# Latent attention in a decoder layer: one exponential over four key blocks, in a pair of PSUM banks

## The chip, the cores and the metric

The kernel runs on all 8 cores of one Trainium2 chip. Each core computes one eighth of the tokens: four cores share a batch element, and each of them owns 16 of its 64 blocks of 128 tokens. The cores don't talk to each other. The metric is the device time in microseconds of the slowest core.

Engines as the profile names them: PE is the matrix engine (PEld its weight loads), ACT is ScalarE, DVE is VectorE, POOL is GpSimd, SP issues the DMAs.

## What is computed

The reference is a decoder layer: RMS norm, one input projection, four retention heads beside eight heads of multi-head latent attention (MLA), an output projection, a SwiGLU feed-forward part and a gated per-layer embedding. The change touches the attention alone, which is this, for each of the 8 heads (query and key 96 wide, value 64 wide, sequence 8192):

```python
s = jnp.einsum('bhqd,bhkd->bhqk', qi, kt).astype(jnp.float32) * scale
mask = kpos[None, :] <= qpos[:, None]
s = jnp.where(mask[None, None], s, -1e30)
pr = jax.nn.softmax(s, axis=-1).astype(vt.dtype)
return jnp.einsum('bhqk,bhkd->bhqd', pr, vt)
```

## The kernel before

**How the program is written.** One Python function, `build_program`, emits five instruction streams. Every operation names the buffers that it reads and writes, and a small tracker adds a semaphore wait where a buffer's last writer or reader is on another engine. Each engine runs its own stream strictly in the order in which the program adds operations. The eight PSUM banks (128 partitions x 512 fp32) are eight separate buffers, `banks[0]` to `banks[7]`; `bank()` (L332) hands out banks 0 to 5 in turn. All matmuls are recorded at L361, in the helper `MM`, whatever they compute, so that they are told apart by shape.

**Stages.** First input projection and retention; then the attention, which is what the change touches, about 1.0 ms; then output projection, feed-forward and embedding, behind a barrier.

**Attention.** The outer loop runs over 4 pairs of heads (`hp`). For each pair it projects keys, values and queries of both heads (L880 to L923), and then works through *rounds*: a round is one head `a` (0 or 1) and one group `g` (0 to 7) of 256 own queries. A round covers `nkb = 8 * (g + 1)` key blocks of 128; the last 8 of them lie at the diagonal and get a mask. There are 64 rounds, with 2304 key blocks in all.

A round is cut into *steps* of two key blocks. For each step:

- `emit_S`: for each block one matmul 96*128, 96x256 (scores, transposed: keys on partitions, 256 queries along the row), into half a bank. For a masked block a second matmul 128*128, 128x256 adds the mask to it.
- `emit_rest`: one exponential on ACT (L963) over the bank, 128x512 from PSUM into a bf16 tile `PTS[t % 4]`; then for each block one matmul 128*65, 128x256 that accumulates values times probabilities (and, in row 64, the denominator) in `acc`, bank 6 or 7.
- Behind a round's last step: a copy of `acc` on ACT (L968), and a reciprocal of the one row of denominators on DVE (L969).
- `emit_F2`, some steps later: one fp32 matmul 1*64, 1x256 (two passes on PE) that spreads the reciprocal over 64 partitions, into a bank from `bank()`, and a multiply on DVE (L953 or L956) that reads it.

The order on PE comes from this loop, where `LOOK = 2`:

```python
for t in range(len(steps)):
    if t + LOOK < len(steps):
        emit_S(t + LOOK)
    for pf in pendF:
        pf[0] -= 1
    while pendF and pendF[0][0] <= 0:
        _, fg, fa = pendF.pop(0)
        emit_F2(fg, fa)
    fin = emit_rest(t)
    if fin is not None:
        pendF.append([2, fin[0], fin[1]])
```

So PE's stream is: scores of step t+2, value matmuls of step t, scores of step t+3, value matmuls of step t+1, and so on, without a break from one round to the next.

Of the kernel before, what the change touches and what calls it, by code (L numbers as in the profile page):

```python
# [6 lines left out]
F32 = mybir.dt.float32  # L7
# [258 lines left out]
def build_program(debug=False, ng_run=NG, stop=None):  # L266
# [567 lines left out]
    cosT = A.f32(2048); sinT = A.f32(2048); csTb = Buf("csT")  # L834
    am = A.bf(8 * 256); amb = Buf("am")
    am3 = am.rearrange("p (i q) -> p i q", i=8)
    PTS = [(A.bf(512), Buf("PTa%d" % i)) for i in range(4)]
    onrm = A.bf(256); onrmb = Buf("onrm")
    o_sb = A.f32(256); o_sbb = Buf("o_sb")
    rden = A.f32(256); rdenb = Buf("rden")  # L840
# [53 lines left out]
    for hp in range(4):  # L894
        KTs = [(KT_A, KT_Ab), (KT_B, KT_Bb)]
        for a in range(2):
            h = 2 * hp + a
            KT, KTb_ = KTs[a]
            for tt in range(16):
                ps, pb = bank()  # L900
                for kc in range(2):
                    MM(ps[0:64, :], pb, w_ukv3[:, kc, h * 128:h * 128 + 64], ck3[:, kc, tt * 512:(tt + 1) * 512], [w_ukvb, ckvnTb], start=(kc == 0), stop=(kc == 1))
                evac_copy(KT[0:64, tt * 512:(tt + 1) * 512], ps[0:64, :], [pb], [KTb_])
        for b4 in range(16):
            ps, pb = bank()
            for j in range(4):
                blk = b4 * 4 + j
                for kc in range(2):
                    MM(ps[:, j * 128:(j + 1) * 128], pb, ck3[:, kc, blk * 128:(blk + 1) * 128], wkv4[:, kc, 2 * hp:2 * hp + 2, 1, :], [w_ukvb, ckvnTb], start=(kc == 0), stop=(kc == 1))
            evac_copy(Vp4[:, b4 * 4:(b4 + 1) * 4, :, 0:64], ps.rearrange("p (j a d) -> p j a d", j=4, a=2), [pb], [Vpb])  # L910
        for a in range(2):
            h = 2 * hp + a
            for tt in range(4):
                p1, p1b = bank()
                p2, p2b = bank()
                for kc in range(3):
                    MM(p1[0:96, :], p1b, w_uq3[:, kc, h * 96:(h + 1) * 96], cq3[:, kc, tt * 512:(tt + 1) * 512], [w_uqb, cqnTb], start=(kc == 0), stop=(kc == 2))
                for kc in range(3):
                    MM(p2[0:96, :], p2b, w_rot3[:, kc, h * 96:(h + 1) * 96], cq3[:, kc, tt * 512:(tt + 1) * 512], [w_rotb, cqnTb], start=(kc == 0), stop=(kc == 2))
                ACT(lambda e, p1=p1, a=a, tt=tt: e.activation(out=QT3[0:64, a, tt * 512:(tt + 1) * 512], in_=p1[0:64, :], func=AF.Copy, scale=SM_SCALE), r=[p1b], w=[QTb])  # L920
                V(lambda e, p1=p1, tt=tt: e.tensor_tensor(out=u1[64:96, :], in0=p1[64:96, :], in1=cosT[64:96, tt * 512:(tt + 1) * 512], op=ALU.mult), r=[p1b, csTb], w=[ub])
                V(lambda e, p2=p2, tt=tt: e.tensor_tensor(out=u2[64:96, :], in0=p2[64:96, :], in1=sinT[64:96, tt * 512:(tt + 1) * 512], op=ALU.mult), r=[p2b, csTb], w=[ub])
                V(lambda e, a=a, tt=tt: e.tensor_tensor(out=QT3[64:96, a, tt * 512:(tt + 1) * 512], in0=u1[64:96, :], in1=u2[64:96, :], op=ALU.add), r=[ub], w=[QTb])  # L923
        steps = []
        for g in range(NG):
            nkb = 8 * (g + 1)
            for a in range(2):
                acc, accb = banks[6 + (acc_i["n"] % 2)]
                acc_i["n"] += 1
                for kp in range(nkb // 2):  # L930
                    steps.append((g, a, kp, nkb, acc, accb))
        LOOK = 2
        sbanks = {}

        def emit_S(t):
            g, a, kp, nkb, acc, accb = steps[t]
            KT, KTb_ = KTs[a]
            s_ps, s_b = bank()
            sbanks[t] = (s_ps, s_b)
            for j in range(2):  # L940
                blk = 2 * kp + j
                diag = blk >= 8 * g
                MM(s_ps[:, j * 256:(j + 1) * 256], s_b, KT[0:96, blk * 128:(blk + 1) * 128], QT3[0:96, a, g * 256:(g + 1) * 256], [KTb_, QTb],
                   start=True, stop=not diag)
                if diag:
                    MM(s_ps[:, j * 256:(j + 1) * 256], s_b, ident, am3[:, blk - 8 * g, :], [constb, amb], start=False, stop=True)

        def emit_F2(g, a):
            bc, bcb = bank()
            MM(bc[0:64, 0:256], bcb, ones_t[64:65, 0:64], rden[64:65, :], [constb, rdenb])  # L950
            dst = mlaT3[a * 64:(a + 1) * 64, hp, g * 256:(g + 1) * 256]
            if a == 0:
                V(lambda e: e.tensor_tensor(out=dst, in0=o_sb[0:64, :], in1=bc[0:64, 0:256], op=ALU.mult),  # L953
                  r=[o_sbb, bcb], w=[mlaTb])
# [343 lines left out]
```

How the kernel before makes its waits and increments, by code:

```python
            def run(e, name):  # L184
                for op in ops[name]:
                    for w in op.waits:
                        e.wait_ge(w.sem, w.val)
                    if op.fn is None:
                        continue
                    ins = op.fn(e)
                    if op.is_dma:
                        ins.then_inc(op.sem, 16)
                    elif op.signal:
                        ins.then_inc(op.sem, 1)
                if name == "sync":
                    for val, sem in finals:
                        e.wait_ge(sem, val)
```

## Time and profile before

| what | us |
|---|---|
| median of 3 runs | 3528.14 (3528.1 to 3564.88) |
| the profiled execution, device time | 3529.14 |
| its span on the slowest core (core 7) | 3526.5 |
| spans of the other cores | 3505.3 to 3521.4 |

Share of the span in which each engine is busy, on the slowest core: PE 66%, ACT 48%, DVE 38%, POOL 13%.

How to read it: the page gives busy time of each engine over the whole span, and the attention is less than a third of it. What a change inside the attention is worth has to be read in its own stretch, from what each engine waits for there. Times of single instructions are start and duration; a start is counted from the beginning of the span. Matmuls overlap: one lasts longer than the distance to the next, and what counts for throughput is the distance.

### The profile page before, as it was taken

How to read it: one execution, taken by the hardware profiler on the slowest of the kernel's cores; microseconds unless marked ns; L12 is line 12 of the kernel's file. 1: busy time of each engine (PE TensorE's matmuls, PEld its weight loads, DVE VectorE, ACT ScalarE, POOL GpSimd, SP SyncE). 2: the span in 40 equal slices, each digit the busy share in tenths (PEclk: the TensorE clock that was granted, in tenths of full speed). 3: DMA queues.
4: the chain of work that ended last, by engine and by line, in shares of the span. 5: the costliest groups of instructions: out<-in, count | busy, mean ns of one | idle time of the engine just before them, and what ended most of it. 6: DMA issues, size and time to landing. Idle time of an engine off the chain costs nothing.

```text
span 3526.5 us, 54269 instructions; the slowest of 8 cores (3505.3 to 3526.5 us)
## 1 busy us (share of the span) xinstructions
PE 2332.3 (66%) x17168; PEld 1486.3 (42%) x17168; DVE 1344.5 (38%) x2716; ACT 1694.8 (48%) x3444; POOL 469.5 (13%) x440
## 2 busy tenths in 40 slices
PE   1656656556566357886886887874332878778776
PEld 0333333333333125654654654651112656556653
DVE  3755757657565442123123123112231222222222
ACT  3655546556454226765765764762222333333333
POOL 0433434334344200000000000000000000000000
PEclk9777778778777678898999998886666988889888
DMA  5111101111010100000000000006443000000000
GB/s 169 43 33 39 42 31 42 30 37 49 31 36 31 19 1 1 1 1 1 1 1 1 1 1 1 1 16 250 183 149 133 15 28 15 28 28 15 29 28 22
DMA packets 40088, 139.58 MB, mean 40 GB/s; under 512 B 7937, under 2 KB 10369, under 8 KB 38786
## 3 DMA queue, kind: packets, MB, share of 16 engines
q1 hardware_dynamic: 38994, 134.47, 11.3%
q0 software_dynamic: 816, 1.64, 0.3%
q8 instruction: 145, 2.38, 0.3%
q14 instruction: 133, 1.09, 0.1%
HBM read 120.96 MB, written 16.78 MB: 39 GB/s over the span
## 4 chain that ended last, share of the span: by engine, by line
PE 41%; DVE 21%; ACT 14%; issue 10%; DMA 8%; POOL 4%; DVEq 1%; SPq 1%; ACTq 0%; POOLq 0%
PE ps L361 38%; DVE arena L969 3%; ACT arena L415 3%; PE ps L366 3%; ACT arena L594 2%; DMA arena<-hs 2%; DMA arena<-w_up 2%; ACT arena L575 1%; DMA hs<-arena 1%; DMA arena<-w_down 1%; DVE arena L891 1%; POOL arena L456 1%; POOL arena L453 1%; ACT arena L963 1%; DMA arena<-w_in 1%
## 5 line engine op out<-in xcount | busy, mean ns | idle before, releaser
L361 PE MATMUL ps<-arena 128*128 128x128 bf16 (+7 forms) x15776 | 2204.8, 299 | 666.4 <-POOL arena L456 222.4
L361 PEld LDWEIGHTS ps<-arena 128*128 128x128 bf16 (+4 forms) x15776 | 1369.3, 108 | 1479.7 <-issue 1119.6
L963 ACT ACTIVATE arena<-ps 128x512 bf16<-128x512 f32 x1152 | 621.8, 596 | 164.3 <-PE ps L361 143.6
L366 PE MATMUL ps<-arena 128*128 128x128 bf16 (+1 forms) x1392 | 161.6, 280 | 516.7 <-DVE arena L1140 172.7
L969 DVE RECIPROCAL arena<-arena 1x256 f32<-1x256 f32 x64 | 111.7, 1745 | 654.2 <-ACT arena L968 654.2
L366 PEld LDWEIGHTS ps<-arena 128*128 128x128 bf16 (+1 forms) x1392 | 123.2, 129 | 548.9 <-issue 546.5
L1175 POOL TENSOR_TENSOR arena<-arena 128x1024 f32<-128x1024 f32 x16 | 37.6, 2348 | 2252.7 <-DVE arena L1173 2252.7
L1157 DVE TENSOR_TENSOR arena<-arena,ps 128x128 bf16<-128x128 f32 x352 | 101.4, 288 | 273.7 <-ACT arena L1156 206.5
L1156 ACT ACTIVATE arena<-ps 128x128 f32<-128x128 f32 x352 | 98.2, 279 | 220.8 <-DVE arena L1157 202.8
L575 ACT COPY arena<-ps 128x1024 bf16<-128x1024 bf16 x80 | 80.4, 1005 | 191.3 <-PE ps L366 191.3
L453 POOL TENSOR_TENSOR arena<-arena 128x512 f32<-128x512 f32 x80 | 102.4, 1280 | 525.3 <-ACT arena L594 525.3
L415 ACT ACTIVATE arena<-arena 128x1024 bf16<-128x1024 f32 x96 | 101.4, 1056 | 141.0 <-DMA arena<-hs 140.9
L420 DVE RECIPROCAL arena<-arena 128x1 f32<-128x1 f32 x224 | 35.9, 160 | 316.7 <-ACT arena L419 315.4
L594 ACT ACTIVATE arena<-ps,arena 128x128 f32<-128x128 f32 x384 | 139.8, 368 | 29.3 <-POOL arena L455 1.2
L889 ACT CAST arena<-ps 64x512 bf16<-64x512 f32 (+1 forms) x96 | 55.0, 581 | 120.9 <-DVE arena L891 68.2
L456 POOL TENSOR_TENSOR arena<-arena 128x512 bf16<-128x512 f32 x80 | 105.6, 1320 | 29.1 <-POOL arena L455 11.2
L415 ACT ACTIVATE arena<-ps 128x512 bf16<-128x512 f32 (+2 forms) x176 | 89.5, 508 | 40.5 <-PE ps L361 30.3
L476 ACT ACTIVATE arena<-arena 128x1408 bf16<-128x1408 f32 (+2 forms) x22 | 36.0, 1637 | 135.0 <-DMA arena<-w_gate 78.2
L891 DVE CAST arena<-ps 64x512 bf16<-64x512 f32 (+1 forms) x96 | 65.1, 685 | 70.0 <-PE ps L361 50.9
L442 ACT ACT_TABLE_LOAD x23 | 29.5, 1283 | 119.7 <-DVE arena L439 119.6
L419 ACT ACT_TABLE_LOAD x64 | 82.1, 1283 | 9.6 <-DVE arena L418 5.8
L419 ACT ACTIVATE arena<-arena 128x1 f32<-128x1 f32 x224 | 66.0, 295 | 35.2 <-DVE arena L418 21.7
(121 smaller groups left out, 1652.7 us busy)
## 6 DMA issues: line engine op xcount, KB each, us to landing
arena<-x_all SPq DMA_DIRECT2D x64, 512.0 KB, 3.5
arena<-x_own SPq DMA_DIRECT2D x32, 512.0 KB, 3.6
arena<-w_gate SPq DMA_DIRECT2D x16, 704.0 KB, 6.3
arena<-w_up SPq DMA_DIRECT2D x16, 704.0 KB, 8.8
arena<-w_down SPq DMA_DIRECT2D x22, 512.0 KB, 4.2
arena<-w_in SPq DMA_DIRECT2D x8, 1360.0 KB, 10.3
hs<-arena SPq DMA_DIRECT2D x16, 512.0 KB, 2.6
arena<-hs SPq DMA_DIRECT2D x16, 512.0 KB, 4.1
```

The costliest lines, as they stand in the source:

```text
L361: return P.add("tensor", lambda e: e.matmul(out_ap, lhsT=lhsT, rhs=rhs, start=start, stop=stop), reads=r, writes=[ob], pe_acc=True)
L366: return P.add("tensor", lambda e: e.transpose(out=out_ap, in_=in_ap, identity=idn[0:in_ap.shape[0], 0:in_ap.shape[0]]), reads=list(r) + [ ...
L415: ACT(lambda e, ap=ap, wdt=wdt, j=j: e.activation(out=junk[:, 0:wdt], in_=ap, func=AF.Square, accum_out=st[:, j:j + 1]), r=rd, w=[sb])
L419: ACT(lambda e: e.activation(out=st[:, 2:3], in_=st[:, 0:1], func=AF.Sqrt, bias=epsc, scale=1.0 / n), r=[sb, constb], w=[sb])
L453: add(lambda e: e.tensor_tensor(out=t13, in0=src3, in1=Cb.unsqueeze(1).to_broadcast([128, nh, hd]), op=ALU.mult), list(rd), tbs)
L456: add(lambda e: e.tensor_tensor(out=out3, in0=t13, in1=t23, op=ALU.add), tbs, [wb])
L575: ACT(lambda e: e.copy(out=xt, in_=psb), r=[pb], w=[xtb])
L594: ACT(lambda e, h=h: e.activation(out=kd[:, h * 128:(h + 1) * 128], in_=ps[:, h * 128:(h + 1) * 128], func=AF.Copy, scale=dscale[:, h:h + 1]),
L891: V(lambda e: e.tensor_copy(out=out_ap, in_=in_ap), r=r, w=w)
L963: ACT(lambda e: e.activation(out=pt, in_=s_ps, func=AF.Exp), r=[s_b], w=[ptb])
L969: V(lambda e: e.reciprocal(out=rden[64:65, :], in_=o_sb[64:65, :]), r=[o_sbb], w=[rdenb])
L1157: V(lambda e, ps=ps, fc=fc: e.tensor_tensor(out=actT3[:, fc, :], in0=sgf, in1=ps[:, 128:256], op=ALU.mult), r=[sgfb, pb], w=[actTb])
```

## The change

The eight banks become four pairs of 1024 fp32 columns. A step covers four key blocks (`kq`) in place of two (`kp`), its scores lie in one pair, `pairs[t % 3]`, and one exponential reads both banks. The probability tiles become 3 of 1024 columns instead of 4 of 512. `LOOK` goes from 2 to 1. `emit_F2` gets its bank handed in, the first of the pair that the step before used, and it comes one (larger) step behind the end of a round instead of two (smaller) ones.

```diff
-    banks = [(P.psum("ps%d" % i, [128, 512], F32)[:, :], Buf("ps%d" % i, excl=True)) for i in range(8)]
+    pairs = [P.psum("pp%d" % i, [128, 1024], F32)[:, :] for i in range(4)]
+    banks = [(pairs[i // 2][:, (i % 2) * 512:(i % 2 + 1) * 512], Buf("ps%d" % i, excl=True)) for i in range(8)]
...
-    PTS = [(A.bf(512), Buf("PTa%d" % i)) for i in range(4)]
+    PTS = [(A.bf(1024), Buf("PTa%d" % i)) for i in range(3)]
...
-                for kp in range(nkb // 2):
-                    steps.append((g, a, kp, nkb, acc, accb))
-        LOOK = 2
+                for kq in range(nkb // 4):
+                    steps.append((g, a, kq, nkb, acc, accb))
+        LOOK = 1
         sbanks = {}
 
         def emit_S(t):
-            g, a, kp, nkb, acc, accb = steps[t]
+            g, a, kq, nkb, acc, accb = steps[t]
             KT, KTb_ = KTs[a]
-            s_ps, s_b = bank()
-            sbanks[t] = (s_ps, s_b)
-            for j in range(2):
-                blk = 2 * kp + j
+            p_ = t % 3
+            sbanks[t] = (pairs[p_], [banks[2 * p_][1], banks[2 * p_ + 1][1]])
+            for j in range(4):
+                blk = 4 * kq + j
+                s_ps, s_b = banks[2 * p_ + j // 2]
+                c0 = (j % 2) * 256
                 diag = blk >= 8 * g
-                MM(s_ps[:, j * 256:(j + 1) * 256], s_b, KT[0:96, blk * 128:(blk + 1) * 128], QT3[0:96, a, g * 256:(g + 1) * 256], [KTb_, QTb],
+                MM(s_ps[:, c0:c0 + 256], s_b, KT[0:96, blk * 128:(blk + 1) * 128], QT3[0:96, a, g * 256:(g + 1) * 256], [KTb_, QTb],
                    start=True, stop=not diag)
                 if diag:
-                    MM(s_ps[:, j * 256:(j + 1) * 256], s_b, ident, am3[:, blk - 8 * g, :], [constb, amb], start=False, stop=True)
-
-        def emit_F2(g, a):
-            bc, bcb = bank()
+                    MM(s_ps[:, c0:c0 + 256], s_b, ident, am3[:, blk - 8 * g, :], [constb, amb], start=False, stop=True)
+
+        def emit_F2(g, a, bk):
+            bc, bcb = bk
...
         def emit_rest(t):
-            g, a, kp, nkb, acc, accb = steps[t]
-            s_ps, s_b = sbanks.pop(t)
-            pt, ptb = PTS[t % 4]
-            ACT(lambda e: e.activation(out=pt, in_=s_ps, func=AF.Exp), r=[s_b], w=[ptb])
-            for j in range(2):
-                blk = 2 * kp + j
+            g, a, kq, nkb, acc, accb = steps[t]
+            s_pair, s_bufs = sbanks.pop(t)
+            pt, ptb = PTS[t % 3]
+            ACT(lambda e: e.activation(out=pt, in_=s_pair, func=AF.Exp), r=s_bufs, w=[ptb])
+            for j in range(4):
+                blk = 4 * kq + j
...
-                emit_F2(fg, fa)
+                emit_F2(fg, fa, banks[2 * ((t + 2) % 3)])
             fin = emit_rest(t)
             if fin is not None:
-                pendF.append([2, fin[0], fin[1]])
+                pendF.append([1, fin[0], fin[1]])
```

## Rows read from the trace of the kernel before

**Rows 1.** Page, costliest groups: count, busy us, mean ns; idle before, what ended it.
```profile
L963 ACT ACTIVATE arena<-ps 128x512 bf16<-128x512 f32 x1152 | 621.8, 596 | 164.3 <-PE ps L361 143.6
```
**Rows 2.** Windows, rounds of each head pair: length, busy us (count) by engine, clock.
```profile
1332.40:1546.15 213.75, 186.47 (x1300) 133.86 (x1298) 33.92 (x37) 160.21 (x304) 0.00 (x0) 0.89 0.00 1
1609.78:1817.97 208.19, 181.25 (x1306) 129.57 (x1304) 33.92 (x37) 158.38 (x303) 0.00 (x0) 0.92 0.00 1
1880.62:2087.17 206.55, 179.33 (x1306) 128.68 (x1304) 33.92 (x37) 158.74 (x304) 0.00 (x0) 0.93 0.00 1
2149.47:2365.51 216.04, 189.27 (x1306) 135.84 (x1304) 33.93 (x37) 160.58 (x303) 0.00 (x0) 0.87 0.00 1
```
**Rows 3.** Timeline of single instructions in steady work: start us, duration, what, how many.
```profile
1803.93 0.60 ACT L963 ACTIVATE arena<-ps 128x512 bf16<-128x512 f32 x1
1804.43 0.59 ACT L963 ACTIVATE arena<-ps 128x512 bf16<-128x512 f32 x1
1804.92 0.59 ACT L963 ACTIVATE arena<-ps 128x512 bf16<-128x512 f32 x1
1805.43 0.60 ACT L963 ACTIVATE arena<-ps 128x512 bf16<-128x512 f32 x1
1804.68 0.38 PE L361 MATMUL ps<-arena 128*65 128x256 bf16 x2
1804.78 0.50 PE L361 MATMUL ps<-arena 128*65 128x256 bf16 x3
```
**Rows 4.** Timeline of ACT over one round of 64 key blocks, copy to copy.
```profile
1798.75 0.37 ACT L968 COPY arena<-ps 65x256 f32<-65x256 f32 x1 [0.73 <-PE ps L361]
1799.02 2.09 ACT L963 ACTIVATE arena<-ps 128x512 bf16<-128x512 f32 x4
1802.44 14.80 ACT L963 ACTIVATE arena<-ps 128x512 bf16<-128x512 f32 x28 [1.33 <-PE ps L361]
1817.97 0.37 ACT L968 COPY arena<-ps 65x256 f32<-65x256 f32 x1 [0.73 <-PE ps L361]
```
**Rows 5.** Timeline of the other engines between rounds, same place (and PE before it).
```profile
1794.77 2.40 PE L361 MATMUL ps<-arena 128*128 128x256 bf16 x20
1798.17 0.27 PE L361 MATMUL ps<-arena 128*65 128x256 bf16 x1
1799.22 1.75 DVE L969 RECIPROCAL arena<-arena 1x256 f32<-1x256 f32 x1 [15.88 <-ACT arena L968]
1799.76 0.60 PE L361 MATMUL ps<-arena 128*65 128x256 bf16 x4 [0.99 <-ACT arena L963]
1801.11 0.61 PE L361 MATMUL ps<-arena 1*64 1x256 f32 x2 [0.75 <-DVE arena L969]
1801.65 1.24 PEld L361 LDWEIGHTS ps<-arena 128*65 128x65 bf16 x12 [0.39 <-issue]
1801.90 0.41 DVE L953 TENSOR_TENSOR arena<-arena,ps 64x256 bf16<-64x256 f32 x1 [0.94 <-PE ps L361]
```
**Rows 6.** Windows of a round of 40 and one of 16 key blocks, as rows 2.
```profile
1683.31:1696.61 13.30, 11.48 (x91) 8.24 (x90) 2.38 (x3) 10.81 (x22) 0.00 (x0) 1.00 0.01 2
1898.26:1905.50 7.24, 5.49 (x43) 4.04 (x42) 2.16 (x2) 4.74 (x9) 0.00 (x0) 1.00 0.00 0
```
**Rows 7.** Instructions of other widths, grouped by shape: busy us, mean ns, idle before.
```profile
L575 ACT COPY arena<-ps 128x1024 bf16<-128x1024 bf16 x80 | 80.4, 1005 | 191.3 <-PE ps L366 191.3
L415 ACT ACTIVATE arena<-arena 128x1024 bf16<-128x1024 f32 x96 | 101.4, 1056 | 141.0 <-DMA arena<-hs 140.9
L658 ACT CAST arena<-ps 128x512 bf16<-128x512 f32 x64 | 37.0, 578 | 0.0
```
**Rows 8.** Around a fall of the clock: windows as rows 2, PE and ACT timeline.
```profile
1709.00:1712.00 3.00, 1.46 (x11) 0.67 (x8) 1.62 (x1) 2.27 (x6) 0.00 (x0) 1.00 0.00 0
1712.02:1718.85 6.83, 6.58 (x29) 4.63 (x30) 0.74 (x3) 3.25 (x7) 0.00 (x0) 0.50 0.01 2
1719.00:1727.00 8.00, 8.00 (x70) 6.17 (x68) 0.00 (x0) 7.61 (x15) 0.00 (x0) 1.00 0.00 1
1715.35 0.60 ACT L963 ACTIVATE arena<-ps 128x512 bf16<-128x512 f32 x1 [0.26 <-PE ps L361]
1716.20 0.60 ACT L963 ACTIVATE arena<-ps 128x512 bf16<-128x512 f32 x1 [0.26 <-PE ps L361]
L361 PE MATMUL ps<-arena 128*65 128x256 bf16 x14 | 4.4, 419 | 0.0
```

More of the change, by code:

```diff
@@ L959, in emit_rest @@
         def emit_rest(t):
-            g, a, kp, nkb, acc, accb = steps[t]
-            s_ps, s_b = sbanks.pop(t)
-            pt, ptb = PTS[t % 4]
-            ACT(lambda e: e.activation(out=pt, in_=s_ps, func=AF.Exp), r=[s_b], w=[ptb])
-            for j in range(2):
-                blk = 2 * kp + j
+            g, a, kq, nkb, acc, accb = steps[t]
[4 more added lines that the diff above has]
+                blk = 4 * kq + j
                 MM(acc[0:65, 0:256], accb, Vp4[:, blk, a, 0:65], pt[:, j * 256:(j + 1) * 256], [Vpb, ptb], start=(blk == 0), stop=(blk == nkb - 1))
-            if 2 * kp + 2 == nkb:
+            if 4 * kq + 4 == nkb:
                 ACT(lambda e: e.copy(out=o_sb[0:65, :], in_=acc[0:65, 0:256]), r=[accb], w=[o_sbb])
@@ L982, in build_program @@
                 _, fg, fa = pendF.pop(0)
-                emit_F2(fg, fa)
+                emit_F2(fg, fa, banks[2 * ((t + 2) % 3)])
             fin = emit_rest(t)
             if fin is not None:
-                pendF.append([2, fin[0], fin[1]])
+                pendF.append([1, fin[0], fin[1]])
         for _, fg, fa in pendF:
-            emit_F2(fg, fa)
+            emit_F2(fg, fa, banks[2 * ((len(steps) + 1) % 3)])
     if stop == "ph3":
```

## The prediction

> **What bounds the kernel now.** I read the page first: 1152 exponentials of 0.596 us, 621.8 us busy, idle 164.3 us before them, nearly all until PE [rows 1]. That says that ACT and PE wait for each other, not who sets the pace. The windows of the four stretches of rounds come next [rows 2]: 213.75 + 208.19 + 206.55 + 216.04 = 844.5 us, the only part of the 3526.5 us that the change touches. Everything else (projections, retention, feed-forward) keeps its instructions and I take it as unchanged.
>
> Then the timeline of single instructions in steady work, at clock 1.00 [rows 3]. Here a loop shows. The exponential of step t starts at 1803.93 and ends at 1804.53. Its first value matmul starts at 1804.68, 0.15 later. PE then issues in order: value matmuls at 1804.68 and 1804.78, then the two score matmuls of step t+3, the second of which ends at 1804.78 + 0.50 = 1805.28. The exponential of t+3 starts at 1805.43, another 0.15 later. A burst of four matmuls lasts 0.60 [rows 5], with 0.27 for one alone: the distance is (0.60 - 0.27) / 3 = 0.11. So the loop is
>
> 0.60 (exponential) + 0.15 (to PE) + 3 x 0.11 (to the fourth matmul) + 0.27 (its length) + 0.15 (to ACT) = 1.50 us for three exponentials,
>
> and 1805.43 - 1803.93 is 1.50. ACT alone could do one each 0.49 (1804.92 - 1804.43: they overlap by 0.11), or 1.47 for three. PE needs 4 x 0.11 = 0.44 for a step. So the latency loop, with a depth of `LOOK + 1 = 3` steps, ties with ACT: 0.50 us for two blocks, 2.00 for eight.
>
> A round of 64 blocks at full clock lasts 1817.97 - 1798.75 = 19.22 [rows 4], one of 40 blocks 13.30 and one of 16 blocks 7.24 [rows 6]. With r = blocks / 8 all three fit **2.00 r + 3.26** (19.26, 13.26, 7.26). The 3.26 holds the masked steps (six matmuls each; PE-bound, 20 matmuls in 2.40 us [rows 5]) and the seam between rounds.
>
> **The change, part by part.**
>
> *One exponential for two.* The trace has no 128x1024 exponential. From a 128x512 cast of 0.578 to a 128x1024 copy of 1.005, both from PSUM, is 0.427 more [rows 7]; on 0.597 that gives 1.02. Bounds: 1.005, and 1.056 (the 128x1024 from SBUF); two whole ones, 1.19, if crossing a bank cost a second start. I take 1.02. ACT could then start one each 1.02 - 0.11 = 0.91, against 2 x 0.50 = 1.00 now.
>
> *Four blocks and LOOK = 1.* PE's stream becomes: scores of t+1 (4 matmuls), values of t (4), scores of t+2 (4), values of t+1. The exponential of t+2 waits for scores that stand behind the value matmuls of t, which wait for the exponential of t. The loop has a depth of two steps:
>
> 1.02 + 0.15 + 7 x 0.111 + 0.27 + 0.15 = **2.37 us for two exponentials, eight blocks**, against 2.00.
>
> Before, while PE and the hops ran (0.90 us), two more exponentials (0.98) covered them; now 1.35 us of PE and hops is covered by one exponential, which adds 0.91 to ACT's time. ACT idles for the rest. PE works 16 x 0.111 = 1.78 of 2.37 (75%), before 89%. Three pairs of banks and three probability tiles are enough: their earlier users end a full step before.
>
> By the ScalarE page of the Trainium skill (ScalarE: Activation LUTs, What ACT_TABLE_LOAD costs) an activation with immediate operands has 186 ns of fixed cost, of which back-to-back ones overlap 93, so that each merged pair saves 93 ns, 576 x 0.093 = 54 us, if ACT sets the pace: 3474 us. The trace shows the overlap a little larger (0.11 [rows 3]); what it denies is that ACT would still set the pace, so I give that result the small chance of the first rival below. The Trainium skill (TensorE: Matmul & The Clock Gate, Part 2, step 1) says that matmuls stay in program order and only weight loads are pulled ahead; by that nothing lifts the scores over the waiting value matmuls.
>
> *The seam.* Let C be the start of the copy L968. Now: exponentials at C+0.27 and on, reciprocal at C+0.47 (1799.22) for 1.75, `emit_F2`'s matmul at C+2.36 (1801.11), value matmuls 0.54 later, the next exponential at C+3.69 (1802.44) [rows 4, 5]. Eight blocks were exponentiated in between. After, by hand with the same hops: exponentials at C+0.27 and C+1.18 (scores of both are emitted before), F2 again at C+2.36, because the reciprocal is 1.75 long whatever the step; four value matmuls from C+2.90 to C+3.23. The next scores go to the pair whose first bank F2 wrote. DVE's multiply starts 0.18 after F2's end (1801.11 + 0.61 = 1801.72, 1801.90) and takes 0.41, so it ends at F2 + 1.20 = C+3.56; scores at C+3.71, the fourth ends at C+4.31, exponential at **C+4.47**, again after eight blocks. Then 2.37 for each two steps. In the last two steps the masks add 4 x 0.11 = 0.44 ahead of the first, X; the second comes at X + 1.33 (12 matmuls), its value matmuls at X + 1.33 + 1.02 + 0.15 = X + 2.50, the next copy at X + 2.50 + 0.33 + 0.27 + 0.20 = X + 3.31 (0.20 is 1798.75 less 1798.28 + 0.27). With X = C + 4.47 + 0.44 + (r - 2) x 2.37:
>
> round after = 8.22 + (r - 2) x 2.37 = **2.37 r + 3.48**. So 22.4 for 64 blocks, 15.3 for 40, 8.2 for 16. For r = 1 both formulas run high by the same 0.8 to 0.9, which cancels.
>
> *Sum at full clock.* r summed over 64 rounds is 288. (2.37 - 2.00) x 288 = 106.6; (3.48 - 3.26) x 64 = 14.1; together **+120.7 us**.
>
> *The clock.* Now: 2.00 x 288 + 3.26 x 64 = 784.6, less 6.4 for r = 1, is 778; the stretches take 844.5, so low clock costs 66 us. The granted clocks of rows 2 (0.89, 0.92, 0.93, 0.87) are shares at 2.4 and 1.2 GHz: 2 x (0.11 x 213.75 + 0.08 x 208.19 + 0.07 x 206.55 + 0.13 x 216.04) = 165 us at 1.2 GHz. There exponentials stand 0.85 apart, PE-bound [rows 8], a loss of 0.35 / 0.85 = 0.41 per us; 165 x 0.41 = 68. After, at 1.2 GHz a loop is 1.02 + 0.15 + 7 x 0.213 + 0.42 + 0.15 = 3.23 but PE needs 16 x 0.213 = 3.41: PE-bound as before, so a low us loses only 1.04 / 3.41 = 0.305. How many there are I bound by 165 (as now, 50 us lost) and 330 (double, 101 lost). Falls follow a seam: PE idled 0.99 + 0.75 in one [rows 5], and a stretch that held one, 1.46 busy of 3.00, was followed by clock 0.50 [rows 8]. After, PE idles more in it: 0.44 before the last values, 2.28 until F2, 0.36 until the bank is free. Steady work at 75% should keep 2.4 GHz: the round of 16 blocks, 42 matmuls x 0.11 in 7.24 us or 64%, ran at 1.00 [rows 6]. I take 220 us, 67 lost, so **+1**.
>
> *Nothing else.* F2's fixed bank replaces `bank()`; its cost is the 0.36 above. No DMA moves. DVE's work is unchanged and idle ahead of it.
>
> Total: 120.7 + 1 = +121 or +122. On the profiled execution, 3529.1 (2.6 more than its span): 3650; the median is 1 lower, **3649 us**, 3.4% slower.
>
> **Rivals.**
>
> *ACT sets the pace (faster).* If the scores of t+2 didn't have to wait, 0.91 for 1.00 on the 448 unmasked step pairs: -0.09 x 448 = -40 us, 3488. It decides once the loop is under 2 x 0.91 = 1.83; it is 2.37, and before it ties at 1.50 to the last hundredth. Chance 0.04.
>
> *The loop is shorter than worked out (same).* Eight blocks in at most 2.06: 0.31 less, with hops of 0.15 and 0.15. Against it: every term is a row. 3528 +- 35. Chance 0.05.
>
> *Two banks cost two starts.* An exponential of 1.19: loop 2.54, +0.17 x 288 = +49, 3698. For it: no activation in the trace reads fp32 across two banks (the 128x1024 from PSUM is bf16, one bank). Chance 0.08.
>
> *The low clock stays.* With 75% of the work and longer idle at the seams PE might not come back. All at 1.2 GHz: 3.41 x 288 + about 4.4 x 64 = 1264, +420; a half of that, 3740 to 3800. The Trainium skill (TensorE: Matmul & The Clock Gate, Part 1) has it that throttled is the default and activity releases it. For it: seams. Against it: at 1.2 GHz PE is full, 3.41 over 3.23, and in rows 8 it came back from 0.50 (PE busy 6.58 of 6.83) to 1.00. Chance 0.06.
>
> **Chances and range.** The forecast has 0.77. Its own range: 3649 less 17 (as much low clock as now), less 9 (hops 0.03 shorter), less 6 (1.005) gives 3617; plus 34 (double low clock), plus 11 (1.056), plus 9 gives 3703. With the two-bank rival at 3698 inside, 3612 to 3705 holds it 8 times in 10. A measurement of this kernel can tell about 1% from no change. Faster 0.04, same 0.06, slower 0.90.
>
> **What would show it.** Right: 576 exponentials of about 1.02; in unmasked steps at full clock their starts alternate 0.91 and 1.45, 2.37 for two; before every second one ACT idles until PE; the round of 64 blocks lasts 22.4; first exponential behind F2 at C+4.47; stretches sum to about 966. Wrong: starts 0.92 apart throughout; an exponential of 1.19; a mean clock in the stretches under 0.8; or a change of time outside the attention.

## The result, and the profile after

The changed kernel is slower: the ratio of its undisturbed executions to those of the kernel before is **1.0376** (95% interval 1.0333 to 1.042). Three of the four took 3662.8 to 3663.5 us and one 3684.9 (forecast 3649, range 3612 to 3705), against 3528 to 3538 for most of those of before. In the other six executions, the profiled one among them, the cores of one die or of both took longer at a lower clock (3732 to 3745 us); in the profiled one that was die 0, before and behind the attention (0.70 or 0.71 against 0.76 to 0.79 in the first 1330 us) and not in its rounds, and all that follows is read on core 7, on the other die, the core that was read before.

Cores and dies of the changed kernel, span and granted clock:

```profile
core 3: 3735.2 us, clock 0.759
core 7: 3656.9 us, clock 0.807
die 0 (median of its cores): 3719.5 us, clock 0.762
die 1 (median of its cores): 3658.3 us, clock 0.812
```

Core 7 went from 3526.5 to 3656.9, by 130.4 us. Windows of the changed kernel, the four stretches of rounds (columns as in [rows 2]), and one round of 48 key blocks that ran at full clock throughout:

```profile
1342.78:1585.63 242.85, 193.87 (x1296) 140.85 (x1294) 33.93 (x37) 148.08 (x159) 0.00 (x0) 0.86 0.00 1
1650.10:1889.08 238.98, 190.55 (x1302) 138.41 (x1300) 33.92 (x37) 148.15 (x159) 0.00 (x0) 0.88 0.00 1
1953.38:2196.07 242.69, 194.49 (x1302) 141.54 (x1300) 33.91 (x37) 148.41 (x160) 0.00 (x0) 0.86 0.00 1
2260.37:2500.08 239.71, 189.55 (x1302) 138.66 (x1300) 33.93 (x37) 147.91 (x159) 0.00 (x0) 0.89 0.00 1
...
2373.21:2390.91 17.70, 13.45 (x109) 10.10 (x106) 2.38 (x3) 12.01 (x14) 0.00 (x0) 1.00 0.00 1
```

They sum to 964.2 us against 844.5: +119.7, with ACT less busy (592.6 against 637.9 us) and waiting more. The first exponential comes 10.4 later (1342.78 against 1332.40), the stretches between the rounds hold 4.5 more and what follows 4.2 less, which makes up the 130.4. A part of that belongs to the change: the first exponential of a head pair now waits for the scores of four blocks and comes 2.02 us behind the first score matmul (1648.08, 1650.10 in the second pair), before 1.16 (1608.62, 1609.78), so four times 0.86, or 3.4 us. The rest I count as scatter: the instructions in front of it are the same, and in the experiments below the first exponential of core 7 comes anywhere from 1331 to 1348 us.

Core 7 is the core whose rounds grew least. On the other seven they grew by 122 to 140 us, and the mean of all eight is 133 (836 to 969). What differs from core to core is the low clock: 234 to 269 us of the rounds ran at 1.2 GHz on the cores of the changed kernel, 132 to 166 before (the clock record of each core).

The group of the exponential on core 7 (count, busy, mean ns; idle before), then the timeline of ACT over that round of 48 blocks:

```profile
L966 ACT ACTIVATE arena<-pp 128x1024 bf16<-128x1024 f32 x576 | 576.4, 1023 | 314.3 <-PE pp L362 310.4 <-ACT arena L966 0.2
```

```profile
2373.21 0.37 ACT L971 COPY arena<-pp 65x256 f32<-65x256 f32 x1 [0.95 <-PE pp L362]
2373.48 1.93 ACT L966 ACTIVATE arena<-pp 128x1024 bf16<-128x1024 f32 x2
2377.67 1.94 ACT L966 ACTIVATE arena<-pp 128x1024 bf16<-128x1024 f32 x2 [2.26 <-PE pp L362]
2380.03 1.94 ACT L966 ACTIVATE arena<-pp 128x1024 bf16<-128x1024 f32 x2 [0.43 <-PE pp L362]
2382.40 1.94 ACT L966 ACTIVATE arena<-pp 128x1024 bf16<-128x1024 f32 x2 [0.43 <-PE pp L362]
2384.77 1.94 ACT L966 ACTIVATE arena<-pp 128x1024 bf16<-128x1024 f32 x2 [0.43 <-PE pp L362]
2387.59 1.03 ACT L966 ACTIVATE arena<-pp 128x1024 bf16<-128x1024 f32 x1 [0.88 <-PE pp L362]
2388.93 1.02 ACT L966 ACTIVATE arena<-pp 128x1024 bf16<-128x1024 f32 x1 [0.32 <-PE pp L362]
2390.91 0.37 ACT L971 COPY arena<-pp 65x256 f32<-65x256 f32 x1 [0.95 <-PE pp L362]
```

Before, the same view showed 28 exponentials without a break [rows 4]. Now they come in twos, and behind every two ACT idles 0.43 us until PE: the loop of two steps, 2380.03 to 2382.40 and 2384.77, 2.37 each. PE's side, at the seam and in the loop:

```profile
2375.64 2.76 PE L362 MATMUL pp<-arena 1*64 1x256 f32 x18 [2.19 <-DVE arena L972]
2376.36 0.41 DVE L959 TENSOR_TENSOR arena<-arena,pp 64x256 bf16<-64x256 f32 x1 [0.87 <-PE pp L362]
...
2381.20 1.96 PE L362 MATMUL pp<-arena 128*65 128x256 bf16 x16 [0.41 <-ACT arena L966]
```

PE waits too: 16 matmuls in 1.96, then 0.41 of nothing until an exponential is done. Both engines idle in the same 2.37 us, each for the other.

### The profile page after: what moved, and what is told of

Its sections match the earlier page's. It is cut to its first block, busy times and chain, and to the rows that moved or that the text cites. A ratio compares the mean times of both kernels' runs of the same rounds, so it can differ in the third digit from the quotient of the medians.

```text
span 3735.2 us, 52537 instructions; the slowest of 8 cores (3649.7 to 3735.2 us)
## 1 busy us (share of the span) xinstructions
PE 2524.9 (68%) x17168; PEld 1586.3 (42%) x17168; DVE 1348.7 (36%) x2716; ACT 1649.5 (44%) x2868; POOL 470.9 (13%) x440
## 3 DMA queue, kind: packets, MB, share of 16 engines
q1 hardware_dynamic: 38994, 134.47, 10.4%
q14 instruction: 124, 1.02, 0.1%
## 4 chain that ended last, share of the span: by engine, by line
PE 39%; DVE 21%; ACT 16%; issue 11%; DMA 8%; POOL 3%; DVEq 1%; SPq 1%; ACTq 1%; POOLq 0%
PE pp L362 37%; ACT arena L966 5%; DVE arena L972 3%; ACT arena L416 3%; PE pp L367 2%; DMA arena<-hs 2%; ACT arena L595 2%; DMA arena<-w_up 1%; DMA hs<-arena 1%; DMA arena<-w_down 1%; DVE arena L892 1%; ACT arena L576 1%; DMA arena<-w_in 1%; POOL arena L454 1%; DVEq L187 1%
## 5 line engine op out<-in xcount | busy, mean ns | idle before, releaser
L362 PE MATMUL pp<-arena 128*128 128x128 bf16 (+7 forms) x15776 | 2401.9, 318 | 716.4 <-POOL arena L457 188.5
L362 PEld LDWEIGHTS pp<-arena 128*128 128x128 bf16 (+5 forms) x15776 | 1473.4, 115 | 1619.0 <-issue 1478.4
L966 ACT ACTIVATE arena<-pp 128x1024 bf16<-128x1024 f32 x576 | 577.0, 1023 | 321.5 <-PE pp L362 317.1
L367 PE MATMUL pp<-arena 128*128 128x128 bf16 (+1 forms) x1392 | 156.8, 275 | 482.7 <-DVE arena L1143 143.5
L367 PEld LDWEIGHTS pp<-arena 128*128 128x128 bf16 (+1 forms) x1392 | 119.0, 126 | 518.1 <-issue 514.9
L1160 DVE TENSOR_TENSOR arena<-arena,pp 128x128 bf16<-128x128 f32 x352 | 101.5, 288 | 308.6 <-ACT arena L1159 257.9
L1159 ACT ACTIVATE arena<-pp 128x128 f32<-128x128 f32 x352 | 97.9, 278 | 255.8 <-PE pp L362 221.3
L576 ACT COPY arena<-pp 128x1024 bf16<-128x1024 bf16 x80 | 80.4, 1005 | 189.0 <-PE pp L367 189.0
L595 ACT ACTIVATE arena<-pp,arena 128x128 f32<-128x128 f32 x384 | 139.8, 368 | 29.4 <-POOL arena L456 1.2
L416 ACT ACTIVATE arena<-pp 128x512 bf16<-128x512 f32 (+2 forms) x176 | 89.4, 508 | 50.6 <-PE pp L362 37.5
```

The costliest lines, as they stand in the source:

```text
L362: return P.add("tensor", lambda e: e.matmul(out_ap, lhsT=lhsT, rhs=rhs, start=start, stop=stop), reads=r, writes=[ob], pe_acc=True)
L367: return P.add("tensor", lambda e: e.transpose(out=out_ap, in_=in_ap, identity=idn[0:in_ap.shape[0], 0:in_ap.shape[0]]), reads=list(r) + [ ...
L416: ACT(lambda e, ap=ap, wdt=wdt, j=j: e.activation(out=junk[:, 0:wdt], in_=ap, func=AF.Square, accum_out=st[:, j:j + 1]), r=rd, w=[sb])
L576: ACT(lambda e: e.copy(out=xt, in_=psb), r=[pb], w=[xtb])
L595: ACT(lambda e, h=h: e.activation(out=kd[:, h * 128:(h + 1) * 128], in_=ps[:, h * 128:(h + 1) * 128], func=AF.Copy, scale=dscale[:, h:h + 1]),
L966: ACT(lambda e: e.activation(out=pt, in_=s_pair, func=AF.Exp), r=s_bufs, w=[ptb])
```

## The experiments

Theory: what costs is the depth of the loop ACT to PE to ACT, counted in steps in flight. Rivals: the merged instruction or the pair of banks, the reuse of a bank by F2, the low clock. The kernels were run in groups, each against the kernel before on the same chip, and the ratio is to the kernel before of its own group. That one took mostly 3528 to 3534 us beside e1, e2, e3 and e5b, 3530 to 3550 beside e4, e8, e9 and e10, and 3534 to 3547 beside e5, e6, e11 and e12, so times of different groups can be compared to some 15 us only. All kernels compute the whole layer.

| run | steps | LOOK | undisturbed, us | ratio (95%) | rounds, core 7 | at 1.2 GHz |
|---|---|---|---|---|---|---|
| before | 2 blocks | 2 | 3528 to 3538 | | 844.5 | 165 |
| changed | 4 | 1 | 3663, 3685 | 1.0376 (1.0333, 1.042) | 964.2 | 246 |
| e1_look1_two_blocks | 2 | 1 | 3779 to 3787 | 1.0674 (1.0628, 1.0719) | 1085.8 | 271 |
| e2_quad_look2 | 4 | 2 | 3530 to 3541, 3560, 3582 | 1.0027 (0.998, 1.0074) | 845.9 | 225 |
| e3_quad_f2_own_bank | 4 | 1 | 3659 to 3665, 3689 | 1.0348 (1.0291, 1.0405) | 970.6 | 262 |
| e5b_quad_half_waits | 4, halves | 1 | 3565 to 3574, 3585, 3602 | 1.01 (1.0063, 1.0137) | 876.3 | 211 |
| e5_quad_two_starts | 4 | 1 | 3625 to 3633 | 1.0224 (1.0144, 1.0303) | 930.1 | 251 |
| e6_before_look3 | 2 | 3 | 3501 to 3507 | 0.9871 (0.9794, 0.9947) | 808.5 | 158 |
| e9_before_late_f2 | 2 | 2 | 3441 to 3446 | 0.9729 (0.9697, 0.9762) | 746.8 | 49 |
| e4_quad_look2_late_f2 | 4 | 2 | 3419 to 3421 | 0.9661 (0.963, 0.9692) | 722.1 | 62 |
| e10_before_late_f2_copy_dve | 2 | 2 | 3424 to 3433 | 0.9691 (0.9649, 0.9733) | 717.3 | 14 |
| e8_quad_look2_copy_dve | 4 | 2 | 3410 to 3414 | 0.9637 (0.9606, 0.9668) | 698.4 | 46 |
| e12_before_dve_later_f2 | 2 | 2 | 3375 to 3379 | 0.9512 (0.9438, 0.9586) | 669.2 | 13 |
| e11_quad_look2_dve_later_f2 | 4 | 2 | 3344 to 3345 | 0.9421 (0.9325, 0.9517) | 639.4 | 13 |

The last column is 2 x (1 - clock) x length, summed over the four stretches, as in the prediction; the clock has two digits, so it is good to about 10 us.

### Depth alone, without merging: e1_look1_two_blocks

The kernel before with one line changed:

```diff
-        LOOK = 2
+        LOOK = 1
```

> The kernel before with LOOK = 1 alone (steps of two key blocks, one bank each, nothing merged). Loop theory: the loop of 1.50 us (0.60 + 0.15 + 3 x 0.11 + 0.27 + 0.15) now holds two exponentials instead of three, so four blocks take 1.50 instead of 1.00 and eight take 3.00 instead of 2.00; a round becomes about 3.0 r + 2.4, which is +236 us at full clock: 3765 us, and exponentials in steady work stand 0.49 and 1.01 apart in turn. At 1.2 GHz the loop is 0.60 + 0.15 + 3 x 0.21 + 0.42 + 0.15 = 1.96 for two and PE has work for 1.71 of it, so PE is not full there; if the clock then doesn't come back, up to 4080 us. Rival (ACT's own rate or the size of the exponential is what costs): no step is larger here, so the time stays at 3528 to 3540.

Five exponentials of its steady work, ACT's timeline:

```profile
1930.12 0.60 ACT L963 ACTIVATE arena<-ps 128x512 bf16<-128x512 f32 x1
1930.98 0.60 ACT L963 ACTIVATE arena<-ps 128x512 bf16<-128x512 f32 x1 [0.26 <-PE ps L361]
1931.62 0.60 ACT L963 ACTIVATE arena<-ps 128x512 bf16<-128x512 f32 x1
1932.48 0.60 ACT L963 ACTIVATE arena<-ps 128x512 bf16<-128x512 f32 x1 [0.27 <-PE ps L361]
1933.12 0.60 ACT L963 ACTIVATE arena<-ps 128x512 bf16<-128x512 f32 x1
```

Two exponentials in 1.50 us (1930.12, 1931.62, 1933.12), where [rows 3] have three in the same 1.50. The split is 0.86 and 0.64 here; the 1.01 and 0.49 that I had written occurs too. The loop fixes only the sum. The rounds grew by 241 us, forecast 236, and the time is 3779 to 3787 us (expected 3765). The fear for the clock was wrong: 271 us at 1.2 GHz, not all. So fewer steps in flight cost time by themselves: nothing was merged, and it costs twice what the change does. What the merging costs beside it, this run doesn't say.

### Depth given back: e2_quad_look2, and F2's bank: e3_quad_f2_own_bank

e3 gives F2 the round's own accumulator bank; e2 is e3 with `LOOK = 2` (which needs that bank, since three pairs are then in use):

```diff
-                return (g, a)
+                return (g, a, (acc, accb))
...
-                _, fg, fa = pendF.pop(0)
-                emit_F2(fg, fa, banks[2 * ((t + 2) % 3)])
+                _, fg, fa, fb = pendF.pop(0)
+                emit_F2(fg, fa, fb)
...
-                pendF.append([1, fin[0], fin[1]])
+                pendF.append([1, fin[0], fin[1], fin[2]])
...
```

> The changed kernel with LOOK = 1 kept and only F2 moved to the round's accumulator bank, so that the next scores needn't wait for DVE to read it. Loop theory: the exponential behind F2 comes at C + 4.10 in place of C + 4.47, 0.37 x 64 = 24 us off the changed kernel: about 3637 us, steady work as in the changed kernel (2.37 for two). Rival (the reuse of the pair's bank for F2 is what makes the change slow): back to about 3530 us.

> The changed kernel with LOOK = 2: three steps of four blocks in flight. The spread of the reciprocal (F2) needs a bank of its own then, and goes into the round's own accumulator bank, which is free once it is copied. Loop theory: the loop of 2.37 holds three exponentials, 0.79 each, so that ACT sets the pace at 0.92 for four blocks (before 1.00), PE just under it at 0.89; unmasked starts 0.92 apart. Behind the copy C the fourth exponential comes at C + 4.10, after 12 blocks. A round 1.83 r + 3.24, -50 us on the kernel before: 3478 to 3490 us. Rival (the merged exponential or the pair of banks itself costs): stays slower than before, 3600 or more. Rival (low clock is the cause): 3600 or more as well, since the seams keep their idle time.

e3's seam (timeline):

```profile
2067.13 0.37 ACT L971 COPY arena<-pp 65x256 f32<-65x256 f32 x1 [0.95 <-PE pp L362]
...
2069.66 2.50 PE L362 MATMUL pp<-arena 1*64 1x256 f32 x18 [2.30 <-DVE arena L972]
...
2071.43 1.02 ACT L966 ACTIVATE arena<-pp 128x1024 bf16<-128x1024 f32 x1 [2.10 <-PE pp L362]
```

The exponential behind F2 comes at C + 4.30, in the changed kernel at C + 4.46 (2377.67 - 2373.21). That is 0.16 x 64 = 10 us and not the 24 I expected: F2 itself starts 0.10 later (C + 2.53 against C + 2.43). In the time even that can't be seen (3659 to 3665 us, expected 3637). So e3 missed its number, and the bank's reuse is out as the cause.

e2, windows of its four stretches and its last round of 64 blocks, and ACT's timeline of that round:

```profile
1331.08:1537.37 206.29, 173.07 (x1296) 144.19 (x1294) 33.92 (x37) 143.12 (x160) 0.00 (x0) 0.89 0.00 1
1601.97:1815.12 213.15, 180.30 (x1302) 148.06 (x1300) 33.92 (x37) 143.39 (x159) 0.00 (x0) 0.86 0.00 1
1878.59:2094.89 216.30, 183.44 (x1302) 149.65 (x1300) 33.92 (x37) 143.58 (x160) 0.00 (x0) 0.85 0.00 1
2157.94:2368.10 210.16, 177.23 (x1302) 146.54 (x1300) 33.91 (x37) 143.36 (x160) 0.00 (x0) 0.87 0.00 1
2350.33:2368.10 17.77, 14.91 (x129) 12.93 (x126) 2.16 (x2) 15.35 (x18) 0.00 (x0) 1.00 0.00 1
```

```profile
2350.60 2.84 ACT L966 ACTIVATE arena<-pp 128x1024 bf16<-128x1024 f32 x3
2354.57 10.19 ACT L966 ACTIVATE arena<-pp 128x1024 bf16<-128x1024 f32 x11 [1.13 <-PE pp L362]
```

At full clock the theory holds: eleven exponentials without a break, the round of 64 blocks in 17.77 (worked out 17.88; before 19.22), the fourth exponential at C + 4.24. The steps in flight are what cost the changed kernel its time: with the same merged instruction, and nearly as much low clock (225 against 246 us), the rounds take 845.9 instead of 964.2. But the gain on the kernel before, some 50 us expected, isn't there. The windows say where it went: 225 us at 1.2 GHz against 165. In a low-clock microsecond e2 loses 1 - 1.83 / 3.41 = 0.46 us, the kernel before 0.41, so 104 against 68 us. That is 36 of the 50. The rest, some 15 us, I can't place row by row; the formula 1.83 r + 3.24 runs 0.3 to 0.5 short in rounds of middle length (12.81 for 40 blocks against 12.39), which over 64 rounds is of that size. A second way to the same end: the median lengths of the rounds at full clock, over all eight cores, add up to 750 us for e2 and 779 for the kernel before. So 29 us are gained at full clock, and the low clock takes 96 us (845.9 - 750) against 66.

### Merging undone in the changed kernel: e5_quad_two_starts and e5b_quad_half_waits

Both issue the exponential as two halves; e5's value matmuls wait for both, e5b's each for its own:

```diff
-    PTS = [(A.bf(1024), Buf("PTa%d" % i)) for i in range(3)]
+    PTS = [(A.bf(1024), [Buf("PTa%d" % i), Buf("PTb%d" % i)]) for i in range(3)]
...
-            ACT(lambda e: e.activation(out=pt, in_=s_pair, func=AF.Exp), r=s_bufs, w=[ptb])
+            for hb in range(2):
+                ACT(lambda e, hb=hb: e.activation(out=pt[:, hb * 512:(hb + 1) * 512], in_=s_pair[:, hb * 512:(hb + 1) * 512], func=AF.Exp), r=[s_bufs[hb]], w=[ptb[hb]])
...
-    ... pt[:, j * 256:(j + 1) * 256], [Vpb, ptb], ...
+    ... pt[:, j * 256:(j + 1) * 256], [Vpb] + ptb, ...          (e5)
+    ... pt[:, j * 256:(j + 1) * 256], [Vpb, ptb[j // 2]], ...   (e5b)
```

> The changed kernel with the exponential issued as two of 128x512, all value matmuls waiting for the second: only the merging itself is undone, step size and LOOK = 1 stay. Loop theory: 0.49 + 0.60 = 1.09 in place of 1.02 in the loop, 2.44 for eight blocks, +0.07 x 288 = 20 us on the changed kernel: about 3680 us; together with e5b_quad_half_waits (3570) it says that the wait for the whole four blocks, and not the size of the instruction, is what costs. Rival (the merged instruction is what is slow): back near 3530.

> The changed kernel, order of PE's stream and LOOK = 1 kept, but the exponential is issued as two of 128x512 with a buffer each, so that each waits for its own bank and the value matmuls wait for their own half. Loop theory: two value matmuls start after the first half (0.75), the other two after the second (1.24), the first bank of scores is complete at 1.24 + 3 x 0.11 + 0.27 = 1.84, the next first half at 1.99, against 2.37: 2.00 for eight blocks as in the kernel before. About -0.37 x 288 = -107 on the changed kernel, less what the seam keeps: 3550 us. Rival (lookahead counted in blocks, or the order of PE's stream, is all that matters): no gain, 3660 or more, since there are two starts of ACT again (1.09 in place of 1.02).

ACT's timeline at full clock, both on core 4, e5 (every half from one first half to the one two steps on), then e5b (its first halves at 1427.84, 1429.83 and 1431.81 are two steps apart each):

```profile
1520.44 0.60 ACT L967 ACTIVATE arena<-pp 128x512 bf16<-128x512 f32 x1
1520.92 0.62 ACT L967 ACTIVATE arena<-pp 128x512 bf16<-128x512 f32 x1
1521.68 0.60 ACT L967 ACTIVATE arena<-pp 128x512 bf16<-128x512 f32 x1
1522.18 0.59 ACT L967 ACTIVATE arena<-pp 128x512 bf16<-128x512 f32 x1
1522.66 0.60 ACT L967 ACTIVATE arena<-pp 128x512 bf16<-128x512 f32 x1
```

```profile
1427.84 0.60 ACT L967 ACTIVATE arena<-pp 128x512 bf16<-128x512 f32 x1 [1.92 <-PE pp L362]
...
1429.83 0.60 ACT L967 ACTIVATE arena<-pp 128x512 bf16<-128x512 f32 x1
...
1431.81 0.60 ACT L967 ACTIVATE arena<-pp 128x512 bf16<-128x512 f32 x1
```

e5b is as worked out: 1.98 for eight blocks, and 3565 to 3574 us (expected 3550) in place of 3663, with two starts of ACT and `LOOK = 1` kept. My number for e5 was wrong in sign: it is *faster* than the changed kernel, not 20 us slower (34 us less in the rounds of core 7, 30 to 38 by the times; the ratios, 1.0224 with at most 1.0303 against 1.0376 with at least 1.0333, agree). I had left out that its first half waits for the first bank alone, which is complete two matmuls earlier. With it the loop is 1.09 + 0.15 + 5 x 0.11 + 0.27 + 0.15 = 2.21, and the trace has 1522.66 - 1520.44 = 2.22. So merging costs here even at the same step size: ACT starts 0.22 later, which is more than the 0.07 that it saves, and PE's wait for four blocks at once costs another 0.23 per eight blocks (2.21 to 1.98).

### The kernel before, one step deeper: e6_before_look3

```diff
-        LOOK = 2
+        LOOK = 3
```

> The kernel before with LOOK = 3 alone. Loop theory: the loop of 1.50 holds four exponentials, 0.375 each, so ACT's 0.49 sets the pace: 1.96 for eight blocks against 2.00, 12 us; and one more exponential gets done before F2's stall, up to 0.49 x 64 = 31 us: 3485 to 3515 us. Rival (depth has nothing to do with it): 3532.

3501 to 3507 us (ratio 0.9871, at most 0.9947), inside what was expected; the rounds lost 36 us. ACT's timeline in steady work at full clock:

```profile
2330.65 0.70 ACT L963 ACTIVATE arena<-ps 128x512 bf16<-128x512 f32 x1
2331.13 0.71 ACT L963 ACTIVATE arena<-ps 128x512 bf16<-128x512 f32 x1
2331.61 0.73 ACT L963 ACTIVATE arena<-ps 128x512 bf16<-128x512 f32 x1
```

They are listed as longer than 0.60 and overlap; what counts is the distance. They start 0.48 apart, most often 0.477: that is ACT's own pace, 1.43 for three and 1.91 for eight blocks, not the 0.49 that I had read out of a loop of three. So loop and ACT did not tie in the kernel before. The loop, 1.50, was the bound by 0.07, which is 0.09 for eight unmasked blocks, or some 20 of the 36 us (0.09 x 224, an estimate). The other part is the fifth exponential that gets done before F2's stall (five behind the copy at 2322.66, where [rows 4] have four).

### The seam: e9, e4, e10, e8, e12, e11

The kernel before spends 3.26 us per round outside its steady work, and F2 takes part of it in every one: these runs put F2 later and then take the copy off ACT. e9 is one number in the kernel before (`pendF.append([4, ...` for 2); e4 is e2 with 2 for 1. e8 and e10 add the copy on DVE, into two tiles, which is what e8 changes in e4:

```diff
-    o_sb = A.f32(256); o_sbb = Buf("o_sb")
+    OSB = [(A.f32(256), Buf("o_sb%d" % i)) for i in range(2)]
...
-                ACT(lambda e: e.copy(out=o_sb[0:65, :], in_=acc[0:65, 0:256]), r=[accb], w=[o_sbb])
+                o_sb, o_sbb = OSB[a]
+                V(lambda e: e.tensor_copy(out=o_sb[0:65, :], in_=acc[0:65, 0:256]), r=[accb], w=[o_sbb])
```

e11 and e12 double `rden` in the same way and have F2 at 3 and at 6.

> The kernel before (steps of two blocks, LOOK = 2) with F2 emitted four steps behind the end of a round instead of two. Seam theory: value matmuls of the third step no longer stand behind F2, the fifth exponential comes at about C + 2.3 instead of C + 3.69, some 1.1 us less for 56 of 64 rounds, 62 us, and with less idle PE time at the seam less low clock (10 to 25): about 3450 us. It tells how much of any gain of the runs with merged exponentials is due to the seam and not to the merging. Rival: F2's delay doesn't matter, 3530.

> The run with LOOK = 2 and four-block steps (e2_quad_look2), F2 moved one more step behind the end of a round, so that PE has the value matmuls of the next step and more scores to do while the reciprocal runs. Seam theory: the stall at F2 goes, exponentials stay about 0.92 apart from C + 0.27 on, a round is 1.83 r + 2.3 instead of 1.83 r + 3.2 at full clock, 58 us less than e2_quad_look2; PE idles only about 1.0 us in a seam, so that the low-clock time, 205 to 230 us there, falls to about that of the kernel before (150) or less, another 25: 3445 us. Rival (the clock takes any gain back, whatever the seam is): stays at 3530.

> As e9_before_late_f2, and the accumulator's copy on DVE into one of two tiles, still with unmerged exponentials of two blocks. Seam theory: a round 2.00 r + about 1.6, some 45 us less than e9_before_late_f2 and little low clock left: 3380 to 3420 us. The difference to e8_quad_look2_copy_dve is then what merging the exponentials is worth once nothing else stalls: 0.17 x 288 = 49 us at most if ACT sets the pace, near 0 if PE does (16 x 0.11 = 1.78 for eight blocks plus masks and F2).

> As e4_quad_look2_late_f2, and the copy of the accumulator on DVE instead of ACT, into one of two tiles, so that ACT needn't wait for the last value matmuls of a round before it starts the next round's exponential. Seam theory: ACT no longer idles before the copy (1.0) nor spends 0.37 in it, and PE no longer idles for the exponential behind it; the rounds become PE-bound, 16 x 0.11 r + 0.9 (masks) + 0.54 (F2) and little else: 1.83 r + 1.5, another 50 us less at full clock, and nearly no low-clock time is left in the rounds (up to 60 less): 3350 to 3400 us. Rival (DVE's reciprocal of 1.75 us becomes the bound, or the clock falls anyhow): no better than e4_quad_look2_late_f2.

ACT in e9, then in e4, behind the copy that opens a round of 64 blocks (timelines):

```profile
2260.33 0.37 ACT L968 COPY arena<-ps 65x256 f32<-65x256 f32 x1 [0.73 <-PE ps L361]
2260.60 3.07 ACT L963 ACTIVATE arena<-ps 128x512 bf16<-128x512 f32 x6
2264.19 12.46 ACT L963 ACTIVATE arena<-ps 128x512 bf16<-128x512 f32 x24 [0.53 <-PE ps L361]
```

```profile
2246.79 3.75 ACT L966 ACTIVATE arena<-pp 128x1024 bf16<-128x1024 f32 x4
2250.84 9.27 ACT L966 ACTIVATE arena<-pp 128x1024 bf16<-128x1024 f32 x10 [0.30 <-PE pp L362]
```

In [rows 4] ACT got four exponentials done behind the copy and then idled 1.33; now it gets six done and idles 0.53, or four large ones and 0.30. e9 took 3441 to 3446 (expected about 3450), e4 3419 to 3421 (3445). At full clock I had worked out 62 and 58 us less than the unmoved kernels; the median lengths of the rounds at full clock add up to 53 and 56 less. What comes on top is the clock, 165 to 49 and 225 to 62 us at 1.2 GHz.

e8 missed: 3410 to 3414, expected 3350 to 3400; and so did its twin e10, 3424 to 3433, expected 3380 to 3420. PE's timeline around the seam of e8:

```profile
2170.22 2.95 PE L362 MATMUL pp<-arena 1*64 1x256 f32 x22 [1.20 <-DVE arena L974]
```

With the copy gone from ACT everything in front of F2 is done sooner, and the reciprocal of 1.75 us is late again: PE idles 1.20 in front of F2. The stall taken away in e4 had come back. Hence the last two:

> e8_quad_look2_copy_dve with F2 one more step later (three behind the end of a round) and two tiles for the reciprocal. In that run's trace ACT starts the next round 0.9 after the last exponential, so that F2, two steps behind, comes to the head of PE's stream before the reciprocal of 1.75 us is done: PE idles 1.3 us and the exponentials stand 2.73 apart once in a round. Seam theory: that gap goes; a round of 64 blocks falls from 17.0 to about 15.8 (PE alone: 136 x 0.11 + 0.54 = 15.7), 64 x 1.2 = 77 us in all, and some of the 60 us at low clock goes as well: 3310 to 3340 us. Rival (the seam's rest is the copy, or the clock takes it back): 3400 or more.

> e10_before_late_f2_copy_dve (unmerged, two-block steps) with F2 six of its small steps behind the end of a round and two tiles for the reciprocal. Seam theory: its one gap of 1.98 between exponentials goes, 1.4 x 64 = 90 us: about 3345 us, and what is left over e11_quad_look2_dve_later_f2 is the price of two starts of ACT where nothing else stalls: 0.50 against 0.46 for two blocks, at most 0.17 x 288 = 49 us, less where PE sets the pace.

e11 at the same place, and its windows for a stretch and a round of 64 blocks:

```profile
2146.74 14.51 PE L362 MATMUL pp<-arena 1*64 1x256 f32 x126 [0.19 <-DVE arena L976]
```

```profile
1345.75:1503.32 157.57, 151.96 (x1296) 132.68 (x1294) 40.25 (x53) 136.99 (x144) 0.00 (x0) 1.00 0.01 1
...
2144.32:2160.47 16.15, 15.96 (x141) 14.15 (x139) 2.80 (x4) 15.27 (x18) 0.00 (x0) 1.00 0.00 1
```

3344 to 3345 us (expected 3310 to 3340), 5.8% under the kernel before of its group and the fastest of all: the round of 64 blocks takes 16.15 in place of 19.22, PE busy 15.96 of it. Its unmerged twin e12 takes 3375 to 3379, 30 more than expected. So with `LOOK = 2` in both the large steps are ahead: by 32 us between e11 and e12 (25 in the rounds, mean of eight cores), 17 between e8 and e10, 25 between e4 and e9.

How much of that the merged instruction earns isn't shown, for e12 is not free of the loop. ACT's timeline there, in steady work at full clock (two exponentials lie between):

```profile
2195.00 0.59 ACT L965 ACTIVATE arena<-ps 128x512 bf16<-128x512 f32 x1
...
2196.49 0.60 ACT L965 ACTIVATE arena<-ps 128x512 bf16<-128x512 f32 x1
```

Three in 1.49, the loop again, where e6 has three in 1.43. By the estimate under e6 that alone can be some 20 of the 32 us. Small steps with `LOOK = 3` and a late F2, which would tell the depth from the merging, were not run.

## Why the prediction was right

- **The loop** (2.37 us for two exponentials, eight blocks): measured 2.37. It carried 107 of the forecast 121 us, and e1 and e5b confirm it from both sides. What the prediction had wrong beside it is that loop and ACT tied at 1.50 before: ACT's 0.49 was read inside the loop, and e6 has 0.477.
- **The exponential**: 1.023 us measured, 1.02 taken from a cast and a copy. The rival of two starts, one for each bank, fell: all 576 average 1.023, and 1.19 was its sign.
- **The seam**: the exponential behind F2 at C + 4.46, worked out C + 4.47; the round of 48 blocks 17.70, and 2.37 x 6 + 3.48 = 17.70. A round of 64 blocks at full clock, one of its signs, doesn't occur in the trace; one of 56 took 20.06 (core 6, 1792.80 to 1812.86), worked out 20.07. Two of the terms inside were off and cancelled: F2 came 0.07 later, and the wait for its bank was shorter (scores at F2 + 1.28 rather than + 1.35). As the cause of anything, the bank's reuse was rated too high, as e3 shows.
- **The clock**: I took 220 us at 1.2 GHz and 67 lost. The windows after give 246, and 964.2 less (2.37 x 288 + 3.48 x 64 - 7 for r = 1) = 898 is 66 lost on core 7. The two agree by a cancelling of errors: there was more low clock than taken, and a microsecond of it lost 0.27 and not 0.305. Over all eight cores it didn't cancel: the changed kernel loses 71 us in the mean (969 - 898), the kernel before 57 (836 - 779), so that the clock cost 14 and not 1. This is the term that was sized too small. Steady work stayed at 2.4 GHz, as expected, although PE idled 0.41 in every 2.37 us; the rival of a clock that stays low fell.
- **The sum**: +119.7 us in the rounds of core 7, forecast +121 or +122. That it fits to 2 us is luck: the mean of the eight cores is +133, by the clock. In the span of core 7 it is +130; 3.4 of the other 10.7 us belong to the change (the first exponential of each head pair), which the prediction had taken as nothing. The time is 14 us over the forecast. The clock's 13 and these 3.4 are of that size, but the undisturbed executions left no trace, so it isn't shown that they are the reason.
- **ACT sets the pace**, the rival on the other side, fell with the first idle 0.43 in ACT's timeline. It describes e2 at full clock (eleven exponentials in 10.19 us): it needed a third step in flight.

What the prediction didn't see is the kernel before: it listed the 3.26 us of the seam, with PE idle 0.99 and 0.75 [rows 5], and passed on to the loop. In the place of one matmul lay 98 us of the rounds (844.5 to 746.8 in e9), near half of it as low clock.

## What to carry to other kernels

Before work is merged into larger steps, write down the loop that runs through both engines, in one instruction each and with the hops, and divide it by the steps in flight; larger steps with fewer of them in flight lengthen it by what each now waits for, even if the same amount of data is under way. Keep the depth in steps, or let each half wait for its own half. And look at what stands in the in-order stream behind a slow small operation: here one matmul, two steps later, was worth 98 us of the rounds, and the large steps with `LOOK = 2` at most 32 of the time.

## What the runs showed of the hardware that I had not expected

- An exponential over 1024 fp32 columns in two PSUM banks takes 1.023 us, against 0.596 over one bank: crossing the bank adds no start. The prediction took this at 1.02 from other instructions; here a trace has it.
- Where nothing holds ACT back, exponentials of 128x512 mostly start 0.477 us apart (e6) and those of 128x1024 0.903 or 0.904 (e2, e11).
- The low clock amplifies small idle times of PE. With F2's stall in each round the rounds ran 158 to 271 us at 1.2 GHz, in all eight kernels that had it; with the stall shortened 14 to 62 us, and without it 13 (core 7). e2 lost its whole gain to this. In the clock records of all cores and kernels every fall of the clock within the rounds, 3202 in all, comes 0.1 to 5.1 us behind a copy of the accumulator, around F2's stall; e10 and e12 have none, and their low clock lies ahead of the first copy. The clock-gate page of the Trainium skill (TensorE: Matmul & The Clock Gate, Part 1) has it that activity releases a throttle that is otherwise on; the windows agree, from 0.85 to 0.89 in e2 to 0.98 to 1.00 in e11.
